# Six pairs of gate tiles made ahead of the attention, as seven block products each

## The chip, the cores and the metric

The kernel runs on one core of a Trainium2 chip. The time is device microseconds for one execution of the whole kernel; times are medians of several runs. The engines are named as in the profile: PE is TensorE (PEld its weight loads), DVE is VectorE, ACT is ScalarE, POOL is GpSimd, SP is SyncE, which here only issues transfers. Each engine runs its own instructions in order and waits for the others by semaphores.

## What is computed

Two transformer blocks, one after the other, on 1024 tokens of width 1024, in float32. The change touches the second block. Cut to what matters, the reference does this there:

```python
h = rms_norm(x, norm_mix_pre)                       # 1024 tokens x 1024
proj = h @ w_in                                      # 1024 x 5120
q, k, v, cb, cc, cx, g_att, g_conv = split(proj)     # 3 x 512, 3 x 512, 2 x 1024
o = stick_breaking_attention(heads(q), heads(k), heads(v))      # 8 heads of 64
y_att = o @ w_att_branch
y_conv = (cb * causal_dwconv(cc * cx, conv_mix_w)) @ w_conv_branch
merged = sigmoid(g_att) * y_att + sigmoid(g_conv) * y_conv
x = x + rms_norm(merged @ w_out, norm_mix_post)
# then the FFN: up, a causal convolution, gelu, down

def stick_breaking_attention(q, k, v):   # strictly causal, s < t, in blocks of 128 queries
    z = q @ k.T / 8
    log_keep = where(strict, log_sigmoid(-z), 0)
    later = reverse_cumsum(log_keep) - log_keep
    return where(strict, exp(log_sigmoid(z) + later), 0) @ v
```

## The kernel before

**Precision.** Each float32 product is made of three matmuls: both operands are split into a high part, rounded by a copy, and a low part, the rest, and `three` sums high x high, high x low and low x high in one bank of PSUM. So each operand costs a copy on ACT or POOL and a subtraction on DVE or POOL. For weights POOL does both (`split`, lines L766, L767 and L769): a chunk of 512 KB lies in one of two buffers of `w_staging` and goes to one of four slots of `w_ring`. SP loads chunk n once chunk n - 2 is split, in the order of `ORDER`.

**Units.** The product h @ w_in is made in *units*: one weight chunk gives 128 output features for all 1024 tokens, in two halves of 512 tokens, each half 8 x 3 = 24 matmuls of 128x128 on 128x512. `MIX` lists the units: for each f in 0 to 3 the kinds cc, cx, cb (convolution) and q, k (two heads), and for each f in 0 to 7 the gates ga and gc, 36 units in all. The halves end in banks 6 and 7; ACT copies cc and the gates away (L1972, L1980), stores the gates to HBM, and makes the high parts of q and k (L1906, L1910), whose low parts DVE makes (L2625, L2630); DVE takes cx and cb (L2680, L2684).

**The mixed stage.** The values are made first (`tm_units` at T_V2). Then `mix(AHEAD)` runs 164 matmuls of units, and after it a loop of 64 *steps*, one for each head and tile of 128 queries, in which PE interleaves attention and units. Step i has tile t (going up in even heads, down in odd ones), so t + 1 *blocks* of 128 keys. Per step:

- PE: `stick_attend` in every other step; `mix(first)`; `turn_weights(i - 1, 0)`, transposes of the first four blocks of weights (L1335); `mix(second)`; `turn_weights(i - 1, 1)`, the other blocks, if there are more than four; `stick_scores(i + 2)` (L1319 to L1321); `mix(third)`. The numbers of matmuls first, second, third stand in `SLICES`, computed at build time from a weight for each step, `beside_share`.
- ACT: high part of the turned weights (L1948), the exponential of the weights of step i (L1934), the second high part, and for i + 2 Abs, Exp and Ln of the scores (L1927 to L1929).
- DVE: `exponent(i)`: three passes over the step's blocks, the middle one a scan (L2642, L2643, L2645); a pass of the convolution if one is due (`PASSES`, L2695 and L2698); `weights_lo(i - 1, 0)` and `(i - 1, 1)`, the low parts (L2655); `attended2` (L2663, L2665).

All four turned groups go through one bank, 4: `turn_weights(i, 1)` waits until the low part of `(i, 0)` is taken. At steps 14, 30 and 46 there is a *border*: from the last slice of the step before (24 matmuls) through the first two of this one (24 and 44) the next two heads' q and k are made, all but their first half, and DVE takes them within step 14. The three borders part the loop into four segments of 16 steps.

**After it** come the branch products (`branch`), which need the stored attention, convolution and gates again; out-projection; FFN. The FFN's up-projection already makes pairs of tiles in seven products rather than eight (`fast_pair`): the 2 x 2 blocks are two output tiles by two halves of the tokens, with the contracted 1024 rows in two halves; sums and differences of blocks are made of the weights (POOL, `weight_sums`), of the data (DVE, `difference`, `less_sum`, `less_parts`, into `ffn_in_sums`) and of the products (ACT copies, DVE `whole`). A product has 12 matmuls, a pair 84.

## Time and profile before

| | |
|---|---|
| median of 3 runs | 2030.89 us (2028.95 to 2031.41) |
| the profiled execution, its own time | 2032.65 us |
| its span | 2030.8 us |
| PE busy, weight loads | 98%, 81% of the span |
| DVE, ACT, POOL busy | 63%, 49%, 38% |
| chain that ended last, through PE, DVE, ACT | 83%, 10%, 2% |
| mean granted TensorE clock | 0.996 of full speed |

The span is from the first instruction of the profiled execution to its last; its own time is that of the same execution measured as the runs are. Busy time of PE counts a pipelined matmul for its whole passage, some 0.39 us, while one can start every 0.23 us.

### The profile page before, as it was taken

The page shows a single profiled execution, that of the slowest core. Times are in us where ns is not written, and L with a number is a line of the kernel's source. Part 1 is how long each engine was busy: PE and PEld are TensorE (multiplying, and loading weights), DVE is VectorE, ACT ScalarE, POOL GpSimd, SP SyncE. Part 2 cuts the span into 40 slices and gives each one's busy share as a digit, 9 for nine tenths or more (in the row PEclk, how much of TensorE's full clock was granted, in tenths as well). Part 3 has the DMA queues.
Part 4 walks back from the last instruction along what each step waited for, and adds up shares of the span by engine and source line. Part 5 has one row for each costly group of instructions (what it writes and reads, how often), then busy time and mean ns, then how long its engine had stood idle before and what let it go on. Part 6 is the DMA issues. An engine that isn't in the chain of part 4 may idle for free.

```text
span 2030.8 us, 27546 instructions
## 1 busy us (share of the span) xinstructions
PE 1986.7 (98%) x10172; PEld 1655.1 (81%) x10172; DVE 1271.2 (63%) x1892; ACT 998.6 (49%) x1812; POOL 771.4 (38%) x647
## 2 busy tenths in 40 slices
PE   7999999999999999999999999999999999999997
PEld 7888889999777888888888888887788888877885
DVE  6775758887263475766758655089544444449886
ACT  5442269998142364654646532163544454445453
POOL 2332422223333222232323245318877777750000
PEclk9999999999999999999999999999999999999999
DMA  5212110100332121122212353242222222267654
GB/s 154 67 53 73 62 69 11 51 12 10 98 135 69 52 72 51 47 67 58 79 44 92 120 174 121 97 146 72 75 92 83 73 83 76 79 220 251 222 188 161
DMA packets 165439, 190.77 MB, mean 94 GB/s; under 512 B 9243, under 2 KB 115255, under 8 KB 165319
## 3 DMA queue, kind: packets, MB, share of 16 engines
q1 hardware_dynamic: 140871, 127.59, 20.2%
q10 hardware_dynamic: 24448, 61.62, 8.6%
q8 instruction: 71, 1.16, 0.2%
q14 instruction: 49, 0.40, 0.1%
HBM read 148.28 MB, written 40.89 MB: 93 GB/s over the span
## 4 chain that ended last, share of the span: by engine, by line
PE 83%; DVE 10%; ACT 2%; issue 2%; DMA 1%; POOL 1%; ACTq 0%; DVEq 0%; SPq 0%; POOLq 0%
PE psum L1296 18%; PE psum L923 16%; PE psum L924 16%; PE psum L925 16%; PE psum L1192 3%; PE psum L1204 3%; PE psum L1335 2%; PE psum L1223 1%; PE psum L1224 1%; PE psum L1225 1%; PE psum L1352 1%; DVE softplus_part L2643 1%; PE psum L1351 1%; PE psum L1320 1%; PE psum L934 1%
## 5 line engine op out<-in xcount | busy, mean ns | idle before, releaser
L1296 PE MATMUL psum<-h,w_ring 128*128 128x512 f32 x1728 | 430.5, 399 | 0.7 <-ACT v L1871 0.7
L1296 PEld LDWEIGHTS psum<-h,w_ring 128*128 128x128 f32 x1728 | 314.6, 188 | 67.1 <-ACT v L1871 1.1
L766 POOL TENSOR_TENSOR w_ring<-w_staging,zero 128x8 fp32r<-128x8 f32 x88 | 33.8, 384 | 766.3 <-PE psum L1296 337.9
L769 POOL TENSOR_TENSOR w_ring<-w_staging,w_ring 128x1024 fp32r<-128x1024 f32 (+1 forms) x88 | 223.2, 2536 | 7.3
L2824 DVE TENSOR_TENSOR psum<-psum,product 128x512 f32<-128x512 f32 x80 | 55.7, 698 | 193.8 <-PE psum L925 166.0
L923 PE MATMUL psum<-ffn_in_sums,w_ring 128*128 128x512 f32 x320 | 128.3, 401 | 4.5 <-DVE ffn_in_sums L2798 2.5
L924 PE MATMUL psum<-ffn_in_sums,w_ring 128*128 128x512 f32 x320 | 127.1, 397 | 0.0
L925 PE MATMUL psum<-ffn_in_sums,w_ring 128*128 128x512 f32 x320 | 126.8, 396 | 0.0
L2655 DVE TENSOR_TENSOR stick_w_t<-psum,stick_w_t 128x512 fp32r<-128x512 f32 (+3 forms) x96 | 53.4, 556 | 115.0 <-ACT stick_w_t L1948 114.5
L923 PE MATMUL psum<-w_ring,ffn_split 128*128 128x512 f32 x308 | 122.4, 397 | 0.8 <-POOL w_ring L902 0.7
L925 PE MATMUL psum<-w_ring,ffn_split 128*128 128x512 f32 x308 | 121.8, 396 | 0.0
L924 PE MATMUL psum<-w_ring,ffn_split 128*128 128x512 f32 x308 | 121.7, 395 | 0.0
L1948 ACT ACTIVATE stick_w_t<-psum 128x512 fp32r<-128x512 f32 (+3 forms) x96 | 47.2, 492 | 131.5 <-PE psum L1335 130.5
L923 PE MATMUL psum<-ffn_in,w_ring 128*128 128x512 f32 x272 | 107.9, 397 | 0.7 <-POOL w_ring L887 0.7
L2142 ACT ACTIVATE product<-psum 128x512 f32<-128x512 f32 x80 | 47.9, 599 | 120.5 <-PE psum L925 120.3
L924 PE MATMUL psum<-ffn_in,w_ring 128*128 128x512 f32 x272 | 107.0, 393 | 0.0
L925 PE MATMUL psum<-ffn_in,w_ring 128*128 128x512 f32 x272 | 106.6, 392 | 0.0
L887 POOL TENSOR_TENSOR w_ring<-w_sums,w_ring 128x512 fp32r<-128x512 f32 x60 | 85.5, 1427 | 36.7 <-ACT w_ring L2136 36.7
L767 POOL TENSOR_SCALAR w_ring<-w_staging 128x1016 fp32r<-128x1016 f32 (+1 forms) x88 | 95.3, 1083 | 0.0
L1824 ACT ACTIVATE probs<-psum,minus_max 128x348 f32<-128x348 f32 x192 | 91.7, 552 | 2.3 <-DVE minus_max L2567 1.9
L923 PE MATMUL psum<-u,w_ring 128*128 128x260 f32 (+1 forms) x256 | 88.7, 347 | 3.8 <-POOL w_ring L769 3.0
L1789 ACT ACTIVATE probs_t<-psum 128x512 fp32r<-128x512 f32 x128 | 76.2, 598 | 22.6 <-PE psum L1204 13.9
(355 smaller groups left out, 5462.3 us busy)
## 6 DMA issues: line engine op xcount, KB each, us to landing
w_staging<-in_w_in SPq DMA_DIRECT2D x57, 512.0 KB, 3.9
w_down_raw<-in_w_down SPq DMA_DIRECT2D x66, 256.0 KB, 3.6
w_staging<-in_w_up SPq DMA_DIRECT2D x24, 512.0 KB, 4.1
w_staging<-scratch_ffn_mid SPq DMA_DIRECT2D x45, 256.0 KB, 3.5
scratch_ffn_mid<-ffn_mid SPq DMA_DIRECT2D x22, 512.0 KB, 2.6
ffn_mid_again<-scratch_ffn_mid SPq DMA_DIRECT2D x43, 256.0 KB, 3.4
w_raw<-in_w_up SPq DMA_DIRECT2D x20, 512.0 KB, 5.2
w_staging<-in_w_out SPq DMA_DIRECT2D x16, 512.0 KB, 3.8
```

What stands on the lines that cost most here:

```text
L767: pool.tensor_scalar(hi[:, 0:w], WS[:, s, 0:w], 1.0, 0.0, ALU.mult, ALU.add).then_inc(S["w_hi"], 1)
L769: pool.tensor_tensor(lo[:, 0:width], WS[:, s, 0:width], plain(hi[:, 0:width]), ALU.subtract).then_inc(S["w_split"], 1)
L887: pool.tensor_tensor(lo, raw_operand(m, o), plain(hi), ALU.subtract).then_inc(S["up_lo"], 1)
L923: pe.matmul(dst, sh, mh, start=first, stop=False, skip_group_check=skip_group_check)
L924: pe.matmul(dst, sh, ml, start=False, stop=False, skip_group_check=skip_group_check)
L925: return pe.matmul(dst, sl, mh, start=False, stop=last, skip_group_check=skip_group_check)
L1192: ins = pe.matmul(PB[:, b, 0:KPART], QS[:, h, P * t:P * t + P], k2[:, h // GROUP, KPART * b:KPART * (b + 1)], start=x == 0, stop=x == 1)
L1204: ins = pe.transpose(PB[0:rows, 3 + g, P * (kt % 4):P * (kt % 4) + P], PR[:, i % 2, first:first + rows], IDENT[:, :])
L1296: ins = pe.matmul(mix_bank(h), (sl if x == 2 else sh)[:, P * k:P * k + P], ml if x == 1 else mh, start=m == 0, stop=m == UNIT // 2 - 1)
L1789: act.activation(PT[:, 0, 4 * g:4 * g + 4, P * t:P * t + P], PB[:, 3 + g, :].rearrange("p (k n) -> p k n", n=P), ACT.Copy).then_inc(S["pt_ ...
L1824: act.activation(PR[:, i % 2, KPART * b:KPART * (b + 1)], PB[:, b, 0:KPART], ACT.Exp, bias=NB[:, i % 2:i % 2 + 1], scale=-1.0).then_inc(S[ ...
L2824: v.tensor_tensor(bank, bank, part_copy(m, i), ALU.add).then_inc(S["up_whole"], 1)
```

## The change

Twelve gate units (ga and gc of f 0 to 5) leave `MIX`. ga 7 and gc 7 are made first, ahead of everything (COVERING = 2), ga 6 and gc 6 last; 24 units remain. Between the first two units and cc 0 stand EARLY = 6 pairs of gate tiles, (ga f, gc f), each made in seven products of sums of blocks as the FFN does it, with the same numbering of semaphores going on (`fast_done`, `pair_done`).

- SP: `load_gate_pairs`, at the place of chunk C_MIX + 2 in its order: both chunks of a pair into `w_staging` when POOL is through with the pair before, then the four stores of the pair before, then on with single chunks.
- POOL: only the seven low parts of a pair.
- ACT: seven high parts (`early_hi`) and four copies of products (`early_copy`) a pair, after the high parts of the sums of h.
- DVE: the sums of h2 (the same functions as in the FFN, moved up, reading `A2`), the four weight sums (`early_sums`) and the four sums of products (`early_out`) into `gate_out`.
- The filler of the loop falls from 1564 to 892 matmuls. `SEGMENTS` is (2, 3, 3, 5) for (6, 6, 7, 8), `beside_share` starts from 5 in place of 16, the middle slice is at most half a step's. The borders keep their 24, 24 and 44. The sums over steps 20 to 27 are 179 before and 102 after. The passes of the convolution come two to a step, in steps 1 to 5, 21 to 24, 37 to 40 and 53 to 56.

The diff, cut to its core:

```diff
+EARLY = 6
+GATES = [(kind, EARLY) for kind in ("ga", "gc")]
+BESIDE = CONVS[0][1:] + CONVS[1] + CONVS[2] + CONVS[3] + GATES
+SEGMENTS = (2, 3, 3, 5)
+COVERING = 2
+AHEAD = (COVERING + 3) * UNIT + COVER
...
-    return 16 + 2.3 * stick_width(i) + 0.3 * stick_width(i - 1) - 0.5 * stick_width(i + 2) - 0.7 * attend
+    share = 5 + 2.3 * stick_width(i) + 0.3 * stick_width(i - 1) - 0.5 * stick_width(i + 2) - 0.7 * attend
+    return max(share, 2)
...
-            b = min(m, 8) if stick_width(i - 1) > 4 else 0
+            b = min(m // 2, 8) if stick_width(i - 1) > 4 else 0
...
+        def load_gate_pairs(sp):
+            rows = a["w_in_2"][0].rearrange("(k p) n -> p k n", p=P)
+            for e in range(EARLY + 1):
+                if e == 0:
+                    sp.wait_ge(S["w_split"], C_MIX + COVERING)
+                else:
+                    sp.wait_ge(S["up_lo"], 7 * e)
+                if e < EARLY:
+                    for g in range(2):
+                        first = 3072 + D * g + P * e
+                        sp.dma_start(WS[:, g, 0:WCH].rearrange("p (k n) -> p k n", k=KT), rows[:, :, first:first + P])\
+                            .then_inc(S[f"w_staged{g}"], 16)
+                if e:
+                    for turn, ((g, h), _) in enumerate(OUT_TURN):
+                        sp.wait_ge(S["up_whole"], 4 * (e - 1) + turn + 1)
+                        sp.dma_start(scratch["gates"][g, P * (e - 1):P * e, FW * h:FW * h + FW], GT[:, turn % 2, :])\
+                            .then_inc(S[f"spill{turn % 2}"], 16)
...
+                if c == C_MIX + COVERING:
+                    load_gate_pairs(sp)
...
+            for e in range(EARLY):
+                for o in range(7):
+                    hi, lo = early_slot(o)
+                    pool.wait_ge(S["up_hi"], fast_done(e - EARLY, o))
+                    pool.tensor_tensor(lo, early_raw(o), plain(hi), ALU.subtract).then_inc(S["up_lo"], 1)
+            for j in range(4):
+                c = C_MIX + COVERING + j
+                pool.wait_ge(S["up_used"], fast_done(-1, min(2 * j + 1, A22)))
+                run(c, c + 1, 1)
...
-            mix(AHEAD)
+            mix(COVERING * UNIT)
+            for e in range(EARLY):
+                m = e - EARLY
+                if e == 1:
+                    pe.wait_ge(S["mix_a"], 2 * COVERING)
+                elif e >= 2:
+                    pe.wait_ge(S["up_whole"], 4 * (e - 1))
+                for o in range(7):
+                    if e == 0 and o in (S1, S2, S3, A22):
+                        pe.wait_ge(S["t_lo"], {S1: 1, S2: 2, S3: 3, A22: 4}[o])
+                    pe.wait_ge(S["up_lo"], fast_done(m, o))
+                    if o in (S2, S3, S4):
+                        pe.wait_ge(S["up_copy"], pair_done(m, {S2: 1, S3: 3, S4: 2}[o]))
+                    product(early_slot(o), [moved(o, x, A2) for x in range(2)], early_quadrant(e, product_to(o)), opens(o))
+            mix(AHEAD - COVERING * UNIT)
...
+            for e in range(EARLY):
+                early_copy(e, A11)
+                early_copy(e, S1)
+                if e + 1 < EARLY:
+                    early_hi(e + 1, A11)
+                early_copy(e, S2)
+                if e + 1 < EARLY:
+                    early_hi(e + 1, S1)
+                    early_hi(e + 1, S2)
+                    early_hi(e + 1, A12)
+                early_copy(e, S3)
+                if e + 1 < EARLY:
+                    early_hi(e + 1, S3)
+                    early_hi(e + 1, S4)
+                    early_hi(e + 1, A22)
...
+            difference(0, (0, 1), (0, 0))
+            less_sum(1, (1, 1), 0, 1)
+            sum_lo(1, 0)
+            sum_lo(2, 1)
+            early_sums(0)
+            difference(2, (1, 1), (0, 1))
+            sum_lo(3, 2)
+            less_parts(3, (1, 0), 1)
+            sum_lo(4, 3)
+            for e in range(EARLY):
+                if e + 1 < EARLY:
+                    early_sums(e + 1)
+                for turn in range(4):
+                    early_out(e, turn)
```

## Rows read from the trace of the kernel before

**Rows 1.** The page's busy times: us, share of the span, instructions.

```profile
PE 1986.7 (98%) x10172; PEld 1655.1 (81%) x10172; DVE 1271.2 (63%) x1892; ACT 998.6 (49%) x1812; POOL 771.4 (38%) x647
```

**Rows 2.** Busy time by window: lead, loop, first to last exponent; name, us (instructions).

```profile
650.30:690.30 40.00, 39.31 (x170) 31.33 (x169) 10.50 (x14) 10.40 (x20) 18.99 (x15) 1.00 0.23 66
690.30:1170.10 479.80, 476.66 (x2427) 394.38 (x2427) 323.37 (x439) 260.94 (x435) 130.49 (x96) 1.00 0.22 69
692.70:1155.30 462.60, 459.56 (x2344) 380.56 (x2345) 313.20 (x425) 253.14 (x421) 121.16 (x90) 1.00 0.20 64
```

**Rows 3.** The same view of segment 1: narrow start, wide part, border.

```profile
813.50:827.20 13.70, 13.70 (x70) 11.35 (x70) 11.16 (x22) 7.64 (x16) 3.62 (x3) 1.00 0.16 44
827.20:888.30 61.10, 60.71 (x320) 50.25 (x318) 45.95 (x53) 38.83 (x54) 20.29 (x12) 1.00 0.22 68
...
900.60:932.40 31.80, 31.80 (x155) 26.27 (x154) 14.88 (x29) 12.20 (x27) 7.26 (x6) 1.00 0.18 53
```

**Rows 4.** Waits of DVE in 692 to 1155: us, times, longest.

```profile
DVE stick_w_t L2655 <- ACT stick_w_t L1948: 109.9, 71, 6.0
```

**Rows 5.** Timeline of ACT, two halves of the first unit: start, duration.

```profile
657.70 0.60 ACT L1972 ACTIVATE cc_cx<-psum 128x512 f32<-128x512 f32 x1 [4.50 <-PE psum L1296]
663.27 0.60 ACT L1972 ACTIVATE cc_cx<-psum 128x512 f32<-128x512 f32 x1 [4.98 <-PE psum L1296]
```

**Rows 6.** Timeline of DVE in the FFN: the first sum of two successive pairs.

```profile
1499.42 0.70 DVE L2824 TENSOR_TENSOR psum<-psum,product 128x512 f32<-128x512 f32 x1 [5.38 <-PE psum L925]
...
1518.91 0.70 DVE L2824 TENSOR_TENSOR psum<-psum,product 128x512 f32<-128x512 f32 x1 [5.38 <-PE psum L925]
```

**Rows 7.** Timeline of DVE at the end of the value products.

```profile
652.72 2.80 DVE L2614 TENSOR_TENSOR v_split<-v,v_split 128x512 fp32r<-128x512 f32 x2 [21.52 <-ACT v_split L1918]
```

**Rows 8.** The tile of sums in the FFN: ns min/median/max, starts.

```profile
L2798 DVE TENSOR_TENSOR ffn_in_sums<-ffn_in_sums_raw,ffn_in_sums x4: 2276/2482/3389, 1383.0 to 1417.8; 128x2048 fp32r<-128x2048 f32 x4
...
L2787 DVE TENSOR_TENSOR ffn_in_sums_raw<-ffn_in,ffn_in_sums_raw x1: 4379/4379/4379, 1376.4 to 1376.4; 128x2048 f32<-128x2048 f32 x1
```

**Rows 9.** The page's groups: low parts of the weights' sums on POOL.

```profile
L887 POOL TENSOR_TENSOR w_ring<-w_sums,w_ring 128x512 fp32r<-128x512 f32 x60 | 85.5, 1427 | 36.7 <-ACT w_ring L2136 36.7
```

**Rows 10.** Timeline of POOL: one split of a weight chunk.

```profile
646.63 1.05 POOL L767 TENSOR_SCALAR w_ring<-w_staging 128x1016 fp32r<-128x1016 f32 x1
647.77 2.39 POOL L769 TENSOR_TENSOR w_ring<-w_staging,w_ring 128x1024 fp32r<-128x1024 f32 x1
```

**Rows 11.** DMA issues in 600 to 1170: count, size, median us to landing.

```profile
w_staging<-in_w_in SPq DMA_DIRECT2D x37, 512.0 KB, 3.9
```

**Rows 12.** Busy time, then granted clock (third from the end), behind two idle stretches.

```profile
1420.50:1424.00 3.50, 3.48 (x9) 2.77 (x10) 3.46 (x3) 1.75 (x3) 3.34 (x3) 0.55 0.45 109
...
1433.50:1437.50 4.00, 4.00 (x11) 3.13 (x12) 1.94 (x2) 0.89 (x3) 3.77 (x4) 0.57 0.35 100
```

**Rows 13.** Timeline of PE there; in brackets the idle time before.

```profile
1420.52 0.80 PE L923 MATMUL psum<-ffn_in_sums,w_ring 128*128 128x512 f32 x1 [2.52 <-DVE ffn_in_sums L2798]
...
1433.46 0.47 PE L923 MATMUL psum<-ffn_in_sums,w_ring 128*128 128x512 f32 x1 [1.94 <-POOL w_ring L887]
```

**Rows 14.** Timeline of DVE around one wide step.

```profile
1096.22 0.68 DVE L2655 TENSOR_TENSOR stick_w_t<-psum,stick_w_t 128x512 fp32r<-128x512 f32 x1
...
1097.85 0.42 DVE L2655 TENSOR_TENSOR stick_w_t<-psum,stick_w_t 128x256 fp32r<-128x256 f32 x1 [0.35 <-ACT stick_w_t L1948]
1098.19 1.21 DVE L2642 SCALAR_TENSOR_TENSOR softplus<-psum,softplus_part 128x1024 f32<-128x1024 f32 x1
1099.43 2.29 DVE L2643 TENSOR_TENSOR_SCAN softplus_part<-one,softplus 128x1024 f32<-128x1024 f32 x1
1101.76 1.22 DVE L2645 TENSOR_TENSOR softplus<-psum,softplus_part 128x1024 f32<-128x1024 f32 x1
```

**Rows 15.** Timeline of DVE in a border: k's second half.

```profile
924.85 2.85 DVE L2630 TENSOR_TENSOR k_lo_lo<-psum,k_hi_hi 64x512 fp32r<-64x512 f32 x4 [2.48 <-ACT k_hi_hi L1910]
```

**Rows 16.** Timeline of DVE: the split of the convolution.

```profile
1163.96 7.92 DVE L2736 TENSOR_TENSOR conv_lo<-conv_raw,conv_hi 128x1024 fp32r<-128x1024 f32 x4
```

More of the change, by code:

```diff
@@ L148, in mix_units @@
 def mix_units():
-    out, n = [("cc", 0), ("q", 0), ("k", 0)], 0
+    out, n = [("ga", KT - 1), ("gc", KT - 1), ("cc", 0), ("q", 0), ("k", 0)], 0
     for s, size in enumerate(SEGMENTS):
@@ L197, in beside_done @@
     out, n = {}, AHEAD
-    place = [(-1, 2)] * n + [(i, x) for i, step in enumerate(SLICES) for x, m in enumerate(step) for _ in range(m)]
+    place = [(-2, u) for u in range(COVERING) for _ in range(UNIT)] + [(-1, 2)] * (n - COVERING * UNIT) + [(i, x) for i, step in enumerate(SLICES) for x, m in enumerate(step) for _ in range(m)]
     for u, (kind, f) in enumerate(MIX):
@@ L217, in conv_passes @@
             for tap in range(3):
-                out[step] = (f, h, tap)
-                step += 1
+                out.setdefault(step, []).append((f, h, tap))
+                step += len(out[step]) // 2
+            step += step in out
     return out
@@ L617, in two_block_kernel @@
         w_dram = weight_chunks(a, const)
+        RAW_IN = [sum(16 * len(w_dram[c][1]) for c in range(g, C_MIX + COVERING, 2)) for g in range(2)]
         block = ctx.enter_context(nc.Block())
@@ L853, in _ @@
             gated_lo(PAIRS - 1)
-            run(C_OUT + 4, C_BR, 1)
+            run(C_OUT + 4, C_MIX + COVERING, 1)
+            for x in range(2):
+                staged[x] += 16 * EARLY
+            for e in range(EARLY):
[7 more added lines that the diff above has]
+                run(c, c + 1, 1)
+            run(C_MIX + COVERING + 4, C_BR, 1)
             run(C_BR, C_OUT2, 2)
@@ L936, in transpose_tile, with product_to, opens, product @@
                     ins.then_inc(S["nt_mm"], 1)
+            def product_to(o):
+                return {A11: (1, 1), S1: (0, 1), S2: (1, 1), A12: (0, 0), S3: (1, 1), S4: (0, 1), A22: (1, 0)}[o]
+            def opens(o):
+                return o in (A11, S1, A12, A22)
+            def product(operand, data, bank, start):
+                sh, sl = operand
+                mh, ml = data
+                for k in range(4):
+                    ins = three(PB[:, bank, :], sh[:, P * k:P * k + P], sl[:, P * k:P * k + P],
+                                mh[:, k, :], ml[:, k, :], start and k == 0, k == 3,
+                                skip_group_check=not start)
+                ins.then_inc(S["up_used"], 1)
             def tm_units(t0, units, c0, chunks, ncols, stat, before=None, after=None, follows=False, lead=1,
@@ L1445, in _ @@
                 up_half(s, 1)
-            def product(q, o, bank, start):
-                sh, sl = fast_slot(o)
-                (mh, ml) = (moved(o, x) for x in range(2))
-                for k in range(4):
-                    ins = three(PB[:, bank, :], sh[:, P * k:P * k + P], sl[:, P * k:P * k + P],
-                                mh[:, k, :], ml[:, k, :], start and k == 0, k == 3,
-                                skip_group_check=not start)
-                ins.then_inc(S["up_used"], 1)
             def fast_pair(i, q, sums={}):
@@ new lines, in sum_lo, with early_sums @@
+            def sum_lo(n, op):
+                v.wait_ge(S["t_hi"], n)
+                v.tensor_tensor(TSUM[:, op, 1, :, :], summed(op, 1), plain(TSUM[:, op, 0, :, :]), ALU.subtract).then_inc(S["t_lo"], 1)
+            def early_sums(e):
+                m = e - EARLY
+                if e:
+                    v.wait_ge(S["up_lo"], 7 * e)
+                for g in range(2):
+                    sem, value = early_landed(e, g)
+                    v.wait_ge(S[sem], value)
+                a11, a12, a21, a22 = (early_raw(o) for o in (A11, A12, S1, A22))
+                s2, s3, s4 = (early_raw(o) for o in (S2, S3, S4))
+                v.tensor_tensor(s3, a11, a21, ALU.subtract).then_inc(S["up_sum"], 1)
+                v.wait_ge(S["up_sum"], pair_done(m, 1))
+                v.tensor_tensor(a21, a21, a22, ALU.add).then_inc(S["up_sum"], 1)
+                v.wait_ge(S["up_sum"], pair_done(m, 2))
+                v.tensor_tensor(s2, a21, a11, ALU.subtract).then_inc(S["up_sum"], 1)
+                v.wait_ge(S["up_sum"], pair_done(m, 3))
+                v.tensor_tensor(s4, a12, s2, ALU.subtract).then_inc(S["up_sum"], 1)
@@ new lines, in early_out @@
+            def early_out(e, turn):
+                m, (to, i) = e - EARLY, OUT_TURN[turn]
+                if turn == 0:
+                    v.wait_ge(S["up_copy"], pair_done(m, 1))
+                if turn == 1:
+                    v.wait_ge(S["up_copy"], pair_done(m, 4))
+                else:
+                    v.wait_ge(S["up_used"], fast_done(m, {0: A12, 2: S4, 3: A22}[turn]))
+                stores = 2 * gate_turn(e) + turn // 2
+                v.wait_ge(S[f"spill{turn % 2}"], 16 * stores)
+                v.tensor_tensor(GT[:, turn % 2, :], PB[:, early_quadrant(e, to), :], EPART[:, i, :],
+                                ALU.add).then_inc(S["up_whole"], 1)
```

189 lines of the change are left out of this document (119 added, 70 removed).

## The prediction

> **What bounds the kernel now.** The page first: PE is busy 98% of the span and DVE 63% [rows 1], and the chain that ended last runs for the most part through PE's matmuls. Read alone that says: matmuls are the time, and a matmul saved is time saved. The change acts between the end of the value products (650.3 us) and the first branch product (1170.1), so I read that stretch by windows. It has 40.0 us of units ahead of the attention and a loop of 479.8 us; in the loop PE is busy 476.7, DVE 323.4, ACT 260.9 [rows 2]. Cut at borders between steps, the same view shows more [rows 3]: in the wide part of a segment (steps 20 to 27, tiles of 5 to 8 blocks) DVE works 45.95 of 61.1 us, in the border, where the next two heads' q and k are made, only 14.88 of 31.8. So the loop is bound by PE, but DVE follows close behind. Most of its idle time is spent waiting for ACT's copy of the turned weights, which waits for PE (109.9 us before L2655 [rows 4]). The matmuls of L1296 are what fills PE there: 1564 of them in the loop, written out in SLICES.
>
> **The price of a matmul.** A half unit has 24 matmuls, and the copies of two successive halves start 5.57 us apart [rows 5]: 0.232 us each, 11.13 us a unit. A pair in seven products has 84; the same product of the same pattern in the FFN repeats every 19.49 us [rows 6], again 0.232 each. ga and gc of one f cost 22.26 now, 19.49 then.
>
> **Part by part**, against the profiled execution's own 2032.65 us (span 2030.8; 1.8 above the median of the runs, which I take off at the end).
>
> 1. Fourteen units leave the loop: 1564 filler matmuls become 892 (the new lists evaluated by hand), 672 fewer, 155.8 us of PE. Two of the units (ga 7, gc 7) are made first: +22.3. Six pairs: 6 x 19.49 = +116.9. If PE were the bound everywhere, the sum would be -16.6.
>
> 2. Start of the pairs: +1. DVE is idle for 21.5 us before 652.7 [rows 7] and makes its first sums of h2 there; from about 652, when ACT comes to their high parts, the rest follows: two high and two low parts 9, the weight sums 3, then a difference and less_parts of three passes each, every sum with its high and low part: some 27, at passes of 2.5 to 3.1 us [rows 8]. The last low part lies ready at about 691. PE wants it after 22.3 + 6 products of 2.8, also at 691. Zero to 4; in the FFN, PE waited 2.52 for the same operand [rows 13]. The first pair's weights, loaded from the end of the second split at 650.2, are early by far.
>
> 3. Inside the pairs, at nothing. POOL has seven low parts of 1.43 us in 19.5 [rows 9]; the weight sums are on DVE (four of about 0.7). SP may load pair e+1 only when POOL has finished pair e, about 2.2 us after PE starts e (ACT 0.6, POOL 1.4), landing 4 to 6 later (3.9 for one of them [rows 11]); in ACT's queue the first high part of e+1 stands ahead of the copy of the S2 product, which PE needs at 11.1 us. That leaves some 2 us. Uncovered, each late microsecond costs six.
>
> 4. Return to single units: +9.0. On SP's queue the four stores of pair 5 stand ahead of the next weight chunk, and the last of them waits for the last sum. After PE's last product: DVE's sum 0.70, SP's two issues about 0.4 each, landing 3.9, then POOL's split 0.2 + 1.05 + 2.39 [rows 6, 10, 11]: 9.0, with nothing for PE to do. Between 7 and 11. After an idle PE the granted clock has been at its lower level, 1.2 GHz: 2.52 us idle before 1420.52, then a mean of 0.55 over 3.5 us, and 0.57 over 4 after 1.94 us idle [rows 12, 13]. One such stretch: +1.7.
>
> 5. The loop. Here the removed work was the cover of DVE's chain, so I sum DVE. It is busy 313.2 us from the first exponent's end (692.7) to the last's (1155.3) [rows 2], and none of this goes away: gates are copied by ACT. The three passes of a step of 8 blocks take 1.21 + 2.29 + 1.22, the low part of its turned weights 0.68 per four blocks [rows 14]. To this come waits that no filler makes. With more than four blocks, the second low part must wait for the first: DVE, PE's turn, ACT's copy, DVE. At 1096.90 the first ends and the second begins at 1097.85, 0.95 for two blocks [rows 14]; from 0.75 for one to 1.4 for four, 1.07 on average. Eight times a segment, and 0.2 a step of small gaps: 10 us beside each wide part, where DVE then needs 45.95 + 10 = 56. PE needs there 61.1 less 77 matmuls (179 become 102), 43.3. DVE is the bound by 13. Four wide parts: 40. The three narrow steps at each start: 2 each, 8. The falling steps: 2 each and 3 at the end, 9.
>
> The borders stay PE's. (z_e of a step is the end of its exponent on DVE, L2645.) In each, 92 filler matmuls run in one block (24, 24, 44), and DVE waits for q and k [rows 15]. From z_e of step 13 to that of step 16: PE reaches the block after 1.5, 72 matmuls 16.7, turns 0.5, ACT and DVE with k's second half 1.3 + 2.85, the next two exponents with a low part 3.2: 26 instead of 31.8, of which DVE works 14.9 and is idle 11. Three borders: 33.
>
> From z_e 0 to z_e 63: 313.2 + 40 + 8 + 9 + 33 = 403. Before it 2.4 as now, behind it 14.8 less 29 matmuls, 8.1. The loop: 413.7 instead of 479.8, so -66.1. It gives back less than half of the 155.8.
>
> 6. The branch products after the loop: +2. PE arrives 6.7 us nearer to the last step, and DVE's split of the convolution (7.92 for four, now starting 6.2 before the first branch [rows 16]) begins about 4 before and would hold back the third and fourth k. Zero to 6.
>
> Sum: 22.3 + 116.9 + 1 + 9.0 + 1.7 - 66.1 + 2 = +86.8, profiled 2119.4, median 2118.
>
> **The rivals.**
> (a) The waits of point 5 outside the borders vanish, other work slipping into them. The loop is then 2.4 + 313.2 + 33 + 8.1 = 356.7, and the sum +29.8: 2061. For: DVE idles only 2.5 us in the narrow start of a segment [rows 3]. Against: the chain of the two low parts is in the code for every wide step, and its DVE order is fixed.
> (b) Faster: PE stays the bound. The sum is -16.6 + 13.7 = -2.9, 2028; with the terms of points 2, 4 and 6 hidden also, 2014. It decides from a loop of 327 us, in which DVE would be idle for 3 of 316 us between the first and the last z_e (17 of 330 with those terms gone), and the borders alone take 33. For it: PE's 98% [rows 1]. The Trainium skill's page "Perfetto Trace Analysis", section "Identifying the Most-Contended Engine", says to find the bottleneck by occupancy and to work on that engine first; with DVE at 67% of the loop that rule gives this rival. The windows by stretch, cut finer than that rule asks for, speak against it.
> (c) The thinned PE loses its clock often in the loop. At half speed a wide part needs 87 us of PE; with half of it at half speed 58, no more than DVE's 56; with three quarters 69, so +13 in each of four, 2170. For: idle of 1.9 and 2.5 us did it [rows 12, 13]. Against: the idle of a step comes in pieces of 0.5 to 1.5 us, and a halved clock fills them. The Trainium skill's page "TensorE: Matmul & The Clock Gate", section "A second HAM failure mode: psum-queue depth-cycling", warns that frequent short idles between groups of matmuls make the clock swing; the trace of before has no such stretch, for the granted clock is 1.00 through the whole loop [rows 2].
> (d) The pairs run late (point 3), say 2 us each: +12, 2130; inside my range.
>
> **The numbers.** Forecast, with (d) as its tail, 2085 to 2150: 0.66. (a) and what lies between it and the forecast, 2045 to 2085: 0.17. (c), above 2150: 0.12. (b) 0.04, no change 0.01. A measurement of this kernel tells 0.2% (4 us) from no change. Range 2070 to 2160. Faster 0.04, same 0.01, slower 0.95.
>
> **What the profile after would show.** PE's share falls to about 93%, with its idle time in the loop before L1335, waiting for DVE's low parts and ACT's exponentials; DVE busy about 46 to 50 of a wide part's 56 us, its wait for the copies of turned weights down from 110 to some 60 us; borders near 26 from z_e to z_e. The pairs 19.5 us apart with PE full; a hole of about 9 us between the last pair and the first unit of the loop's lead, and a dip of the clock behind it. A loop under 370 us would refute the sum of waits, one of 328 the whole argument; a second clock level all through the loop would say (c). What could make me wrong most: the average wait of a wide step, where 0.5 us more or less moves the time by 16.

## The result, and the profile after

The changed kernel takes 2141.59 us (median of 4 runs, 2137.65 to 2144.14), beside 2030.98 for the kernel before in the same job: 1.0543 times as long, interval 1.0529 to 1.0556. The forecast was 2118, its range 2070 to 2160. So it is slower, as said, and by 23.6 us more than said. The profiled execution took 2144.14 (span 2142.3), and the sums below are made against it: 111.5 us more span than before.

The page of the changed kernel, its busy times and its chain by engine:

```profile
PE 2011.3 (94%) x10100; PEld 1665.9 (78%) x10100; DVE 1345.3 (63%) x1955; ACT 1032.0 (48%) x1858; POOL 784.7 (37%) x653
...
PE 74%; DVE 17%; issue 3%; ACT 3%; DMA 2%; POOL 1%; ACTq 0%; SPq 0%; DVEq 0%; POOLq 0%
```

PE's share fell from 98% to 94% [rows 1]. It executes 72 matmuls fewer than before, and is still busy for 24.6 us longer. The windows, in the columns of [rows 2, 3], granted clock third from the end, show where the time goes: the loop from the first exponent to the last, then the narrow start, the wide part and the border of segment 1, the first wide part, and the 10 us after the last pair:

```profile
851.00:1270.00 419.00, 346.25 (x1710) 280.12 (x1710) 316.49 (x425) 238.53 (x394) 61.79 (x48) 0.93 0.12 36
962.20:971.50 9.30, 9.07 (x46) 7.02 (x46) 8.65 (x16) 7.78 (x17) 0.00 (x0) 1.00 0.05 11
971.50:1035.00 63.50, 49.03 (x244) 39.60 (x243) 51.22 (x58) 36.94 (x50) 11.86 (x9) 0.91 0.09 26
1045.10:1072.10 27.00, 26.49 (x127) 21.39 (x126) 14.25 (x26) 12.14 (x27) 7.24 (x6) 1.00 0.15 42
860.60:922.40 61.80, 42.82 (x200) 35.10 (x201) 50.65 (x54) 34.92 (x46) 7.21 (x6) 0.83 0.08 22
802.00:812.00 10.00, 3.79 (x9) 3.05 (x10) 0.00 (x0) 0.00 (x0) 7.08 (x6) 0.51 0.54 151
```

The loop has 634 matmuls fewer than in [rows 2] and is shorter by only 43.6 us. The wide part of segment 1 has 76 fewer than in [rows 3] and takes 63.5 us where it took 61.1: nothing came back there. DVE works 51.2 of it instead of 45.95, and PE is idle for 14.5. Where nothing else binds, in the narrow start and the border, the time fell: 13.7 to 9.3, 31.8 to 27.0.

The waits, of PE in the whole span, then of DVE in the loop (us, times, longest). Line numbers moved: L1385 is the filler (before L1296), L1424 the turns of the weights, L1408 the scores, L2800 the low part of the turned weights (before L2655), L2790 the end of an exponent.

```profile
PE psum L1424 <- DVE stick_w_t L2800: 61.3, 28, 5.2
PE psum L1408 <- DVE softplus L2790: 12.1, 16, 2.0
PE psum L1385 <- POOL w_ring L826: 9.2, 1, 9.2
PE psum L992 <- ACT gate_product L2009: 6.1, 1, 6.1
...
PE psum L992 <- DVE conv_lo L2961: 2.1, 1, 2.1
```

```profile
DVE stick_w_t L2800 <- ACT stick_w_t L2067: 57.0, 54, 2.9
DVE k_lo_lo L2775 <- ACT k_hi_hi L2029: 16.0, 6, 2.8
DVE q_stack L2770 <- ACT q_stack L2025: 13.0, 6, 2.7
DVE conv_y L2829 <- PE psum L1385: 4.9, 4, 2.3
DVE cc_cx L2825 <- PE psum L1385: 3.4, 4, 2.2
```

PE now waits 61.3 us for DVE's low parts, and DVE's own wait for ACT's copies fell from 109.9 us [rows 4] to 57.0: in the wide parts PE and DVE have changed places. One wide step of the changed kernel, in the timelines of DVE and then of PE (start, duration, idle before):

```profile
1006.38 1.22 DVE L2790 TENSOR_TENSOR softplus<-psum,softplus_part 128x1024 f32<-128x1024 f32 x1
1007.52 0.48 DVE L2840 TENSOR_SCALAR conv_y<-cc_cx,vectors 128x512 f32<-128x512 f32 x1
1008.03 0.75 DVE L2843 SCALAR_TENSOR_TENSOR conv_y<-cc_cx,vectors,conv_y 128x512 f32<-128x512 f32 x1
1008.70 0.68 DVE L2800 TENSOR_TENSOR stick_w_t<-psum,stick_w_t 128x512 fp32r<-128x512 f32 x1
1010.77 0.69 DVE L2800 TENSOR_TENSOR stick_w_t<-psum,stick_w_t 128x512 fp32r<-128x512 f32 x1 [1.38 <-ACT stick_w_t L2067]
```

```profile
1009.44 0.66 PE L1424 MATMUL psum<-ident,softplus 128*128 128x128 f32 x4 [3.27 <-DVE stick_w_t L2800]
```

Two passes of the convolution (1.2 us) stand between the exponent and the first low part. PE sits idle for 3.27 us until that low part ends and turns the second four blocks. ACT copies them, and DVE waits 1.38 us for the copy: the chain of the two low parts, of point 5, in its longest form.

The lead has two holes. Timelines of ACT, PE, SP and POOL in the changed kernel, around the start of the pairs and around their end:

```profile
683.18 1.91 ACT L1987 ACTIVATE ffn_in_sums<-ffn_in_sums_raw 128x2048 fp32r<-128x2048 f32 x1 [6.93 <-DVE ffn_in_sums_raw L2873]
685.00 1.06 ACT L2009 ACTIVATE gate_product<-psum 128x512 f32<-128x512 f32 x2
...
685.72 0.76 PE L992 MATMUL psum<-ffn_in_sums,w_ring 128*128 128x512 f32 x1 [6.09 <-ACT gate_product L2009]
...
808.21 4.21 PE L1385 MATMUL psum<-h,w_ring 128*128 128x512 f32 x9 [9.22 <-POOL w_ring L826]
...
794.81 5.26 SPq L690 DMA_DIRECT2D scratch_gates<-gate_out  x3
800.11 12.06 SPq L728 DMA_DIRECT2D w_staging<-in_w_in  x4
...
804.53 0.20 POOL L823 TENSOR_TENSOR w_ring<-w_staging,zero 128x8 fp32r<-128x8 f32 x1 [22.98 <-issue]
804.70 1.04 POOL L824 TENSOR_SCALAR w_ring<-w_staging 128x1016 fp32r<-128x1016 f32 x1
805.82 2.34 POOL L826 TENSOR_TENSOR w_ring<-w_staging,w_ring 128x1024 fp32r<-128x1024 f32 x1
```

At the first, ACT's copies of the first pair's products stand behind `sum_hi(4, 3)`, for whose operand ACT waited 6.93 us. At the second, the first single chunk is loaded at 800.1, behind the last pair's stores.

### The profile page after: what moved, and what is told of

Its sections match the earlier page's. It is cut to its first block, busy times and chain, and to the rows that moved or that the text cites. A ratio compares the mean times of both kernels' runs of the same rounds, so it can differ in the third digit from the quotient of the medians.

```text
span 2142.3 us, 27550 instructions
## 1 busy us (share of the span) xinstructions
PE 2011.3 (94%) x10100; PEld 1665.9 (78%) x10100; DVE 1345.3 (63%) x1955; ACT 1032.0 (48%) x1858; POOL 784.7 (37%) x653
## 4 chain that ended last, share of the span: by engine, by line
PE 74%; DVE 17%; issue 3%; ACT 3%; DMA 2%; POOL 1%; ACTq 0%; SPq 0%; DVEq 0%; POOLq 0%
PE psum L992 17%; PE psum L994 17%; PE psum L993 17%; PE psum L1385 7%; PE psum L1279 3%; DVE softplus_part L2788 3%; PE psum L1291 3%; PE psum L1310 1%; PE psum L1311 1%; PE psum L1312 1%; PE psum L1424 1%; DVE softplus L2787 1%; DVE stick_w_t L2800 1%; DVE softplus L2790 1%; DVE ffn_in_sums L2877 1%
## 5 line engine op out<-in xcount | busy, mean ns | idle before, releaser
L1385 PE MATMUL psum<-h,w_ring 128*128 128x512 f32 x1152 | 312.1, 416 | 9.9 <-POOL w_ring L826 9.2
L823 POOL TENSOR_TENSOR w_ring<-w_staging,zero 128x8 fp32r<-128x8 f32 x76 | 22.2, 292 | 800.1 <-PE psum L1385 306.4
L1385 PEld LDWEIGHTS psum<-h,w_ring 128*128 128x128 f32 x1152 | 217.6, 198 | 54.1 <-POOL w_ring L826 9.7
L826 POOL TENSOR_TENSOR w_ring<-w_staging,w_ring 128x1024 fp32r<-128x1024 f32 (+1 forms) x76 | 195.0, 2566 | 6.3
L992 PE MATMUL psum<-ffn_in_sums,w_ring 128*128 128x512 f32 x416 | 166.8, 401 | 10.5 <-ACT gate_product L2009 6.1
L993 PE MATMUL psum<-ffn_in_sums,w_ring 128*128 128x512 f32 x416 | 165.3, 397 | 0.0
L994 PE MATMUL psum<-ffn_in_sums,w_ring 128*128 128x512 f32 x416 | 165.3, 397 | 0.0
L1424 PE MATMUL psum<-ident,softplus 128*128 128x128 f32 x288 | 51.8, 291 | 61.5 <-DVE stick_w_t L2800 61.3
L992 PEld LDWEIGHTS psum<-ffn_in_sums,w_ring 128*128 128x128 f32 x416 | 79.2, 190 | 30.3 <-issue 6.7
L1424 PEld LDWEIGHTS psum<-ident,softplus 128*128 128x128 f32 x288 | 36.8, 147 | 83.7 <-DVE stick_w_t L2800 75.4
L994 PEld LDWEIGHTS psum<-ffn_in_sums,w_ring 128*128 128x128 f32 x416 | 79.3, 191 | 19.3
L993 PEld LDWEIGHTS psum<-ffn_in_sums,w_ring 128*128 128x128 f32 x416 | 79.5, 191 | 18.3
```

Of the source, the lines that this page charges most:

```text
L826: pool.tensor_tensor(lo[:, 0:width], WS[:, s, 0:width], plain(hi[:, 0:width]), ALU.subtract).then_inc(S["w_split"], 1)
L992: pe.matmul(dst, sh, mh, start=first, stop=False, skip_group_check=skip_group_check)
L993: pe.matmul(dst, sh, ml, start=False, stop=False, skip_group_check=skip_group_check)
L994: return pe.matmul(dst, sl, mh, start=False, stop=last, skip_group_check=skip_group_check)
L1385: ins = pe.matmul(mix_bank(h), (sl if x == 2 else sh)[:, P * k:P * k + P], ml if x == 1 else mh, start=m == 0, stop=m == UNIT // 2 - 1)
L1424: ins = pe.transpose(PB[:, 4, P * (kt % 4):P * (kt % 4) + P], ZS[:, i % 3, P * kt:P * kt + P], IDENT[:, :])
```

## The experiments

Loop means first to last exponent, lead the time from the first matmul of a unit to the end of the first exponent, both in the profiled execution. The last column is the median's distance from the median of the kernel that was edited, taken as 2141.6 for the changed kernel and 2030.6 for the one before. The ratio is to the kernel before in the same job. Filler is the matmuls of the single units left beside the attention.

| kernel | filler | lead | loop | median us | ratio (interval) | distance |
|---|---|---|---|---|---|---|
| before | 1564 | 40.9 | 462.6 | 2030.98 | 1 | |
| changed | 892 | 199.5 | 419.0 | 2141.59 | 1.0543 (1.0529 to 1.0556) | |
| e1_orders | 892 | 182.0 | 417.8 | 2124.95 | 1.0466 (1.0449 to 1.0484) | -16.6 |
| e2_more_filler | see text | 198.9 | 422.7 | 2148.91 | 1.0586 (1.0568 to 1.0603) | +7.3 |
| e3_sum_between | 892 | 199.2 | 411.8 | 2134.57 | 1.0515 (1.0497 to 1.0532) | -7.0 |
| e4_dve_load_after | 892 | 199.3 | 461.1 | 2185.9 | 1.0768 (1.075 to 1.0786) | +44.3 |
| e5_dve_load_before | 1564 | 40.9 | 517.7 | 2085.64 | 1.0272 (1.0255 to 1.0289) | +55.0 |
| e6_both_orders | 892 | 182.0 | 410.6 | 2115.15 | 1.0413 (1.0396 to 1.0431) | -26.4 |
| e7_two_pairs | 1276 | 102.0 | 414.2 | 2040.82 | 1.005 (1.0033 to 1.0067) | |
| e8_sum_between_before | 1564 | 40.9 | 458.6 | 2026.01 | 0.9979 (0.997 to 0.9989) | -4.6 |
| e9_even_load_before | 1564 | 40.9 | 489.3 | 2057.28 | 1.0123 (1.0108 to 1.0139) | +26.7 |
| e10_even_load_after | 892 | 200.8 | 461.3 | 2190.59 | 1.0773 (1.0754 to 1.0791) | +49.0 |
| e11_one_pair | 1372 | 82.6 | 431.9 | 2039.81 | 1.0042 (1.0028 to 1.0055) | |
| e12_four_pairs | 1084 | 142.8 | 394.2 | 2061.48 | 1.0148 (1.0132 to 1.0163) | |

**The two holes of the lead.** On SP the last pair's stores go behind two more chunks. On ACT the last high part goes behind three copies.

```diff
-                if e:
-                    for turn, ((g, h), _) in enumerate(OUT_TURN):
...
+                if 0 < e < EARLY:
+                    store_gate_pair(sp, e - 1)
...
+                if c == C_MIX + COVERING + 2:
+                    store_gate_pair(sp, EARLY - 1)
...
             early_hi(0, A22)
-            sum_hi(4, 3)
...
+                if e == 0:
+                    early_copy(e, S2)
+                    sum_hi(4, 3)
```

> The changed kernel with two orders of issue mended and nothing else: on SP the stores of the last pair stand behind the next two weight chunks, on ACT the high part of the fourth sum of h2 stands behind the copies of the first three products of pair 0. My account of the lead says: the 9.2 us hole of PE before L1385 is only SP's order, and the 6.1 us hole before L992 is only ACT's order (the copy that PE wants stands behind a wait for DVE's fourth sum). Both go, with most of the clock's loss behind them: 14 to 18 us less, 2125 to 2128; the loop stays at 419 us from the first z_e to the last. Rival: the holes are limits of the data (the sums of h2, a weight chunk's landing and split), and other waits come in their place: less than 5 us gained, 2137 to 2142.

The lead fell by 17.5 us and the time by 16.6: both orders cost what their holes show, with the low clock behind them, and all of it lies on the path.

**Is PE or DVE the bound in the wide parts?** The filler's matmuls with a low part (x = 1, 2; two in three) are issued a second time in steps of over four blocks, so the units made there hold these parts doubled:

```diff
+                    if x and m < UNIT // 2 - 1 and stick_width(at_step) > 4:
+                        pe.matmul(mix_bank(h), (sl if x == 2 else sh)[:, P * k:P * k + P], ml if x == 1 else mh,
+                                  start=False, stop=False)
```

> The changed kernel; in the loop's steps with more than four blocks every unit's matmul of a low part is issued a second time (two more for each k, but for the last; the low parts are then counted twice, so the product is very slightly off). That is some 70 matmuls more in each wide part, 270 in all, 62 us of PE work. DVE's chain bounds the wide parts (my account): a wide part has 12 to 19 us in which PE is idle, so most of the work disappears in them and the loop grows by 5 to 25 us; if the lowered clock of these parts was what cost more than my sum, it grows least, since PE is busier and keeps its clock. Rival, PE is the bound everywhere: the time grows by the full 62 us, to 2203.

The windows of that kernel: its loop, the first wide part, that of segment 1.

```profile
849.60:1272.30 422.70, 386.26 (x1958) 314.50 (x1958) 314.92 (x425) 239.06 (x394) 63.12 (x48) 0.97 0.12 36
859.20:916.60 57.40, 47.44 (x250) 38.64 (x251) 48.66 (x53) 35.24 (x46) 8.50 (x6) 0.94 0.09 24
965.60:1032.10 66.50, 59.80 (x307) 49.05 (x306) 51.42 (x58) 37.09 (x51) 11.87 (x9) 0.97 0.09 25
```

248 matmuls more in the loop, 57.5 us at 0.232, and the loop grew by 3.7. The median of the whole grew by 7.3, for the profiled execution was the fastest of the four (2142.16, the others 2148.0 to 2150.3). Either way PE is not the bound. The first wide part even became 4.4 us shorter, with the clock at 0.94 instead of 0.83.

**The chain of the two low parts.** In DVE's order, the sum over the attended heads goes between the two low parts, into the time in which DVE waits for the copy:

```diff
                 evacuate((i, 1))
-                if i:
-                    weights_lo(i - 1, 1)
                 if i >= 3 and i % 2 and not late_sum(i):
                     attended2((i - 3) // 2)
+                if i:
+                    weights_lo(i - 1, 1)
                 evacuate((i, 2))
```

> The changed kernel with one order on DVE changed: the two passes that take the attention's result (0.84 us, every other step) stand between the two low parts of the turned weights rather than behind the second. My account says that DVE is idle for about 1.1 us between the two low parts in every wide step and that DVE's chain is the period: 16 wide steps then lose 0.6 to 0.84 us each, 10 to 13 us less, 2128 to 2132. Rival, PE or the clock sets the wide steps' period: no change, within 3 us; or slower, because the second low part is what PE waits for next.

> The changed kernel with the mended orders of SP and ACT (which gave 16.6 us) and with DVE's two passes between the low parts (7.0 us). The one acts ahead of the loop and the other inside it, so they add: 23 to 24 us less than the changed kernel, 2117 to 2120. If both gains come from the same thing, the clock for instance, it is less than 19.

> The kernel before with DVE's two passes of the attention's result between the two low parts, the order that gave 7.0 us on the changed kernel. Here PE is the bound and DVE's gaps lie beneath it: within 3 us of before. If DVE's chain already set the wide steps here, 5 to 10 us less.

The same edit gives 7.2 us of loop in the changed kernel, less than the 10 to 13 expected, and 4.0 in the kernel before. The direction is that of the chain. The size falls short since most of the gain (5.1) came in the first wide part and little in the next three (0.3, 1.1, 1.8). And 1.9 of the 5.1 are DVE's own busy time there (50.65 before, 48.76 after): a scan that had run beside POOL's split took 2.36 us instead of 3.96, which is no part of the chain. Together with the orders of the first experiment it adds up, and a little more: -26.4 beside -23.6, 2 us below what was expected. On the kernel before it gives the only version that beats both: 0.9979, small but outside its interval. I had expected it within 3 us of no change, and was wrong by little.

**Work added to DVE.** Two useless additions a step, ahead of the low part, once in each kernel. First with two operands in SBUF:

```diff
+                if g == 0:
+                    for x in range(2):
...
+                        v.tensor_tensor(XTRA[:, :], plain(A2[:, 0, 0, 0:256]), plain(A2[:, 0, 1, 0:256]), ALU.add).then_inc(S["extra"], 1)
```

> The changed kernel with two useless additions of 128x256 on DVE before the first low part of every step (0.42 us each, with their gaps 0.9 to 0.95 a step, 60 us in all). If DVE's chain is the bound outside the borders, 55 of the 64 steps are longer by all of it: 45 to 58 us more, 2187 to 2200. If PE were the bound, DVE has 24% of the loop idle and the time grows by less than 15 us.

> The kernel before with the same two useless additions on DVE in every step as in the run that gave +44.3 us on the changed kernel. By windows DVE is close behind PE here too: a wide part needs 46 + 10 + 8 = 64 us of DVE's chain against 61 to 68 of PE, a narrow start 11 + 2 + 3 = 16 against 14, the borders have room. I expect 8 to 25 us more, 2038 to 2055, a third of what the changed kernel paid. If PE alone bounds it: less than 4 us. If DVE's chain were the bound here already, as in the changed kernel: 40 us or more.

The first came in at the edge of what was expected, +44.3 where 45 to 58 was said. The second missed by far: +55.0 where 8 to 25 was expected. The tile of the additions in that kernel (ns min/median/max) and its timelines of DVE and POOL around one place show why:

```profile
L2658 DVE TENSOR_TENSOR extra<-h x128: 412/424/2655, 694.1 to 1214.2; 128x256 f32<-128x256 f32 x128
```

```profile
713.23 3.10 DVE L2658 TENSOR_TENSOR extra<-h 128x256 f32<-128x256 f32 x2
716.25 0.68 DVE L2661 TENSOR_TENSOR stick_w_t<-psum,stick_w_t 128x512 fp32r<-128x512 f32 x1
...
713.11 2.47 POOL L770 TENSOR_TENSOR w_ring<-w_staging,w_ring 128x1024 fp32r<-128x1024 f32 x1
```

The load was not the same in both kernels. 33 of the 128 additions of e5 met POOL's work on weight chunks and averaged 1.42 us; in the changed kernel, which splits fewer chunks there, 7 did. DVE's busy time grew by 79.7 us in one and by 52.4 in the other. So the pair was made again with one operand in PSUM and one in SBUF, behind the wait for the copy, where each took at most 0.43 us:

```diff
+                        v.tensor_tensor(XTRA[:, 0:P * min(w, 2)], PB[:, 4, 0:P * min(w, 2)], plain(A2[:, 0, 0, 0:P * min(w, 2)]), ALU.add)
```

> The load of 44 and 55 us was not the same on the two kernels: an addition with two operands from SBUF took 0.42 us alone and up to 2.65 beside POOL's subtraction, and POOL splits twice as many chunks in the loop of before (DVE's busy time grew by 79.7 us there, by 52.4 on the changed kernel). Here the two useless additions take one operand from PSUM, so they should take 0.42 (0.29 for one block) whatever POOL does: about 53 us with gaps. Kernel before: a wide part's chain becomes 46 + 12.5 + 7 = 65.5 against 61, 61, 68, 60 of PE, the narrow and falling parts grow by 1 each: 18 to 28 us more. If DVE's chain bounds this kernel fully, 45 or more; if PE does, less than 5.

> The same even load on the changed kernel: outside the borders all of it shows, 38 to 48 us over 2141.6, so 2180 to 2190, about twice what the kernel before pays. If both kernels pay the same, the balance of PE and DVE is the same in both and my account of before is wrong.

Loops of the kernel before and of the changed one with this load:

```profile
695.30:1184.60 489.30, 467.06 (x2350) 381.08 (x2351) 359.47 (x550) 253.60 (x421) 120.99 (x90) 1.00 0.20 61
```

```profile
854.20:1315.50 461.30, 358.02 (x1710) 287.62 (x1710) 361.77 (x550) 240.22 (x394) 60.14 (x48) 0.90 0.11 34
```

46.3 us more of DVE's work lengthen the loop before by 26.7; 45.3 us lengthen the changed one by 42.3 (the median of the whole by 49.0, 1 us above what was expected). Before, some two fifths of it disappeared beneath the filler. After the change hardly any does: DVE's chain is the bound nearly everywhere. That even the kernel before pays 58% shows how close to that chain it already stood.

**How many pairs?** All three with the orders of e6; the gate units left are spread between those of the convolution, which puts its units and passes at other steps:

```diff
-EARLY = 6
+EARLY = 2
-SEGMENTS = (2, 3, 3, 5)
+SEGMENTS = (5, 5, 5, 6)
-    share = 5 + 2.3 * stick_width(i) + 0.3 * stick_width(i - 1) - 0.5 * stick_width(i + 2) - 0.7 * attend
+    share = 10 + 2.3 * stick_width(i) + 0.3 * stick_width(i - 1) - 0.5 * stick_width(i + 2) - 0.7 * attend
```

The same with 1 pair, (5, 6, 6, 6), 12; and with 4 pairs, (4, 4, 4, 5), 8.

> The kernel of all three mended orders with two early pairs rather than six; eight gate units are back in the loop (27 units there, SEGMENTS 5, 5, 5, 6, the share starting from 10). PE then has 1276 matmuls in the loop, 413 us of work, and DVE's chain about the same. Ahead of the loop it costs 22.3 + 39.0 + 2, and the loop falls by about 50 (to some 430, since both are tight), so 2035 to 2055, slower than before by 0.2 to 1.2%. If PE is the bound as long as it is 95% busy, the sum is -5.6 + 3: 2028. If time lost goes by the pairs (88 us for six with all orders mended), 2058.

> All mended orders with one early pair; 29 units in the loop (SEGMENTS 5, 6, 6, 6, share from 12), 1372 matmuls, so PE's floor there is 435 us, above the 421 to 425 that the loop took with 892 and 1276. Then PE is the bound again and each matmul saved counts: ahead of the loop 22.3 + 19.5, in the loop 4 units less, -44.5, with the 2 us at the seams: -1 from one pair, and -4.6 from DVE's order: 2022 to 2030. If the loop cannot be filled as evenly as by hand, up to 2035.

> All mended orders with four early pairs, 23 units in the loop (SEGMENTS 4, 4, 4, 5, share from 8), 1084 matmuls. By the two bounds, the loop stays at DVE's 411 us between the first and last z_e, and the lead costs 39 more than with two pairs: 2076 to 2082. If the loss went by pairs in proportion, it would be 2078 as well, so the total tells little; the loop tells: 409 to 414 by my account, 397 if the loop still fell as it did from six to two pairs counted per matmul of PE.

Loops of one, two and four pairs, and the wide part of segment 1 with four:

```profile
734.60:1166.50 431.90, 421.95 (x2171) 348.56 (x2172) 309.51 (x426) 249.31 (x414) 97.33 (x78) 1.00 0.19 58
```

```profile
753.50:1167.70 414.20, 401.77 (x2078) 329.74 (x2079) 308.07 (x425) 246.32 (x410) 89.72 (x72) 1.00 0.19 56
```

```profile
794.20:1188.40 394.20, 363.13 (x1895) 294.79 (x1895) 309.04 (x426) 243.13 (x402) 76.65 (x60) 1.00 0.16 48
911.10:963.50 52.40, 49.15 (x264) 40.25 (x265) 45.95 (x53) 37.35 (x51) 9.11 (x7) 1.00 0.18 56
```

One pair missed: 2039.81, where 2022 to 2030 was expected from a loop still bound by PE. PE is idle for 9.9 us of that loop, 8.2 of them waiting for DVE's low parts, where in e8 it is idle for 0.9. Four missed on the other side: 2061.48 instead of 2076 to 2082. The loop with four is 394.2 us, near the 397 named for the rival and not the 409 to 414 of my account: the 411 of e3 and e6 was no floor that DVE sets whatever the units do. Two came in as expected.

Against the kernel before with the same DVE order (e8, 458.6 us), the loops of e11, e7, e12 and e6 hold 178, 271, 455 and 640 filler matmuls fewer between the first exponent and the last, and are shorter by 26.7, 44.4, 64.4 and 48.0 us. At 0.232 a matmul that is 65%, 71%, 61% and 32% of PE's time saved. A pair leaves out 96 matmuls, 22.3 us, and costs 19.5 in the lead, so it would need 88% back in the loop to pay, and none of these does. The second pair comes nearest: its loop is 17.7 us shorter for 93 matmuls (82%), and the time 1.0 longer.

## Why the prediction was right, and where its sum was short

Its own steps against the profile. The sum was +86.8 and the span grew by 111.5; of the 24.7 missing, the loop holds 16.0 and the lead 7.4.

**Points 1 and 3, the price of the early work: right.** From the end of the value products to the first exponent the time went from 42.4 to 200.7, +158.3 where the terms of points 1, 2 and 4 give +150.9. The leads of one, two, four and six pairs (82.6, 102.0, 142.8, 182.0) stand 19.4 to 20.4 apart a pair, beside 19.49 in the sum. The pairs don't run late, so rival (d) is out.

**Point 2, start of the pairs: the step was right, its size wrong.** It was put at 1 us, with a range to 4, and the hole is 6.1. I followed PE's operand (the last low part). What came late was the copy of a product, held on ACT's queue behind a high part whose sum DVE had not yet made: a queue in which an early instruction waits for late data, the thing that point 3 looked for inside the pairs and not at their start. The first experiment confirms it.

**Point 4, return to single units: right.** 9.2 us, where 9.0 was summed from queue, landing and split. The granted clock there was 0.51 over 10 us with the hole in it. In e1 this hole is gone and ACT's is 1.9: 13.4 us of idle time, and a lead shorter by 17.5. Of the other 4.1, 3.9 are the low clock behind the two holes, for which 1.7 was in the sum: the first nine intervals between matmuls behind the one and the first ten behind the other are 0.36 to 0.59 us, most of them 0.43, where 0.23 is usual.

**Point 5, the loop: the mechanism was right, the sum of DVE's waits too small.** First to last exponent is 419.0 us where 403 was said. Shown by three kinds of runs: 57.5 us more of PE's work cost 3.7 in the loop (e2); 45.3 to 52.4 of DVE's cost 42.1 to 42.3 (e10, e4); a shorter DVE chain gave 7.2 (e3). Term by term: DVE is busy 316.5 (313.2 taken) and idle 102.5 (90 taken). The narrow starts need 3.5 of idle time, where 8 was given. The falling steps need 12.7 (9) and the borders 39 (33). The wide parts need 47.2 (40), and they also have more to do. That the loop came within 16 us is in part luck, for two errors offset. With DVE's busy time of before in each part, the sum gives the four wide parts 227.9 us and they took 250.7; it gives the narrow starts 52.8 and they took 37.9. The falling steps took 48.5 (45.0) and the borders 81.9 (77.6).

The step that failed is "DVE then needs 45.95 + 10 = 56": it takes DVE's work in a wide part from before. But the change moves the convolution's passes into steps 21 to 24, 37 to 40 and 53 to 56, as the diff says, so that of segment 1 has 51.2 to do, while the narrow start has 8.7 instead of 11.2 [rows 3]. Of the 5.25 more in the wide part, some 2.1 are the passes and 1.4 the two products cc * cx. The rest, 2.1, is something that I had overlooked: a scan of 128x640 took 3.61 us beside POOL's split of a chunk, and 1.49 elsewhere. Four scans of the changed loop lengthened so, by 2.0 to 2.2 each, and all its scans together take 95.4 us where they took 88.3. One of them stands ahead of PE's longest wait, in the first wide part (timelines of DVE, POOL and PE):

```profile
911.64 3.96 DVE L2788 TENSOR_TENSOR_SCAN softplus_part<-one,softplus 128x768 f32<-128x768 f32 x1
...
911.58 2.41 POOL L826 TENSOR_TENSOR w_ring<-w_staging,w_ring 128x1024 fp32r<-128x1024 f32 x1
...
917.25 0.90 PE L1424 MATMUL psum<-ident,softplus 128*128 128x128 f32 x3 [5.22 <-DVE stick_w_t L2800]
```

A scan of this size takes 1.76 us elsewhere; PE waits for the low part that DVE makes behind it.

And with the filler thin, DVE waits in the wide steps for the units themselves (`conv_y` and `cc_cx`, 4.9 + 3.4 us, where before only 2.6 for `cc_cx`). In this part, 51.2 and 12.3 idle make the 63.5. With four pairs the passes lie behind the borders again, DVE works its 45.95 in the wide part as before, and the part takes 52.4: with 192 matmuls more than e6 and the same order on DVE, the loop is 16.4 us shorter. Of these, 5.2 are DVE's busy time (309.0 instead of 314.3; its scans account for 5.8) and 11.2 its idle time, 8.0 of it in the waits for units (`conv_y` and `cc_cx`, 9.9 us in e6 and 1.9 with four pairs). So in this arrangement the six-pair version is past the point where fewer matmuls help at all. Six pairs with the passes behind the borders were not run.

Open is how much of these 16.4 is the clock. The granted clock was 0.93 in the changed loop and 1.00 with four pairs. In e2 the clock of the first wide part rose from 0.83 to 0.94 and the part fell from 61.8 us to 57.4, but 2.0 of these 4.4 are DVE's busy time (50.65 to 48.66), for the scan shown above took its 1.76 there. That the wide part of segment 1 stayed long in e2, 66.5 us at 0.97, with DVE busy 51.4, says that in the others the arrangement weighs more. And e3 shortened the same first part by 5.1 with the clock at 0.86, so the two are not separated. No run held the arrangement and changed the clock alone.

**Point 6: right** within a microsecond. PE waited 2.1 for the convolution's low parts where 2 was summed; the tail is 8.9 (8.1).

**The rivals.** (a), waits that vanish: out, DVE's idle time in the loop is 102.5 us, more than I gave it. (b), PE stays the bound: out by e2, and with it the reading of 98% on the page. The Trainium skill's page "Perfetto Trace Analysis", section "Identifying the Most-Contended Engine", takes the engine of the highest occupancy, and judges TensorE by its FLOPs and its weight loads rather than by its matmul time. Over the whole span of the changed kernel that still points to PE (weight loads 78%, DVE 63%), and that engine could be given 57.5 us more in the loop at a cost of 3.7 there. In the loop alone the same measure points to DVE (316.5 us, weight loads 280.1), and the runs agree. (The sum of rival (b), 2028, goes with a loop of 324 us, 479.8 less 155.8, and not with the 327 written there; 430.4 was measured.) (c), the clock: in part. It did fall, to 0.83 and 0.91 in the first two wide parts. The argument against it failed: idle pieces of 0.5 to 1.5 us were said, and the longest in these parts were 5.2 and 4.1. But a second clock level all through the loop there was not (the borders had 0.98 and 1.00), and the wide parts took 61.3 to 64.1 us where (c) put 69. The Trainium skill's page "TensorE: Matmul & The Clock Gate", section "A second HAM failure mode: psum-queue depth-cycling", describes such swings behind short idles. The trace agrees that they occur. What they cost is not shown. Of the 859 filler matmuls in the changed loop, 59 took 0.55 us or more where 0.39 is usual; at 0.2 us each, an estimate, that is 12 us of PE's time, in a loop in which PE is idle for 72.8.

## What to carry to other kernels

Before work is taken from the busiest engine, sum the second engine by stage: its busy time plus the waits that its order forces. Where that sum is near the stage's length, the busiest engine is only filling gaps, and each microsecond taken from it returns a part (here 0.6 to 0.7 of it up to 455 matmuls of the loop; the loop without 640 was longer again, though its units also stood elsewhere). Work made cheaper elsewhere must be priced by that returned part: 12% cheaper does not pay at 60 or 70% returned. And when work moves, recount each stage's own load, since the passes that come with a unit weigh most where the engine that makes them is the bound.

Where a new block of work goes between the old orders of several queues, ask what stands behind its first instructions that wait, and what stands behind its last ones. Two reorderings took the holes here from 15.3 us to 1.9.

## What the runs showed of the hardware

A DVE addition of 128x256 with both operands in SBUF took 0.41 to 0.42 us alone and up to 2.65 beside a `tensor_tensor` of 2.5 to 2.9 us on POOL, so it can lose nearly the whole length of that. DVE's scan of 128x768 went from 1.76 to 3.96 in the same way. Which of the two is held up differed: a scan of 128x640 that began 0.24 us ahead of such a POOL instruction kept its 1.50, and POOL's took 3.42 instead of 2.4. With one operand in PSUM (e9) the addition stayed within 0.43, also the 29 times when it ran beside the same POOL instruction. The Trainium skill's page "GPSIMD Engine Reference", section "1. Specifications", names contention of POOL with DVE instructions of two SBUF inputs, without a price; the trace agrees, and this is the price.

The granted clock fell to a mean of 0.83 over a 62 us stretch in which PE was busy for 42.8 and no single wait passed 5.2 us, and to half behind single idle stretches of 2 us: after 2.05 us among the branch products the matmuls of one line took 0.63 instead of 0.39. This shows in the timeline of PE in the changed kernel:

```profile
1283.18 0.54 PE L992 MATMUL psum<-conv_hi,w_ring 128*128 128x512 f32 x1 [2.05 <-DVE conv_lo L2961]
1283.52 0.63 PE L993 MATMUL psum<-conv_lo,w_ring 128*128 128x512 f32 x1
...
1287.17 0.39 PE L993 MATMUL psum<-conv_lo,w_ring 128*128 128x512 f32 x1
```
